# A new order of heavy and light steps, and a small product moved behind a larger one, in a two-layer hybrid decoder trunk

## The reference

```
swiglu(h, wg, wu, wd) = (silu(h @ wg) * (h @ wu)) @ wd
logits = t @ router ; top_v, top_i = top_k(logits, 2) ; top_w = softmax(top_v)
out = sum over experts e of combine[:, e] * swiglu(t, eg[e], eu[e], ed[e])
```

## Time and profile before

| | us |
|---|---|
| median of 3 runs | 1355.4 (1354.23 to 1355.93) |
| the profiled execution | 1358.07 |
| its span, first to last instruction | 1356.1 |
| TensorE busy in the span | 1307.8 |
| VectorE busy | 1139.9 |
| ScalarE busy | 945.6 |
| mean granted clock of TensorE | 0.987 of full |

### The profile page before, as it was taken

How to read it: one execution, slowest core, us unless ns; L and a number is a source line. 1 busy time by engine, 2 the same in 40 slices (tenths; PEclk the granted TensorE clock), 3 DMA queues, 4 the chain that set the end, 5 groups by cost and what they waited for, 6 DMA issues and landing times.

```text
span 1356.1 us, 17180 instructions
## 1 busy us (share of the span) xinstructions
PE 1307.8 (96%) x6502; PEld 1072.6 (79%) x6503; DVE 1139.9 (84%) x1045; ACT 945.6 (70%) x844; POOL 100.0 (7%) x67
## 2 busy tenths in 40 slices
PE   8999999999999999999999999999999999999984
PEld 5898888887898878788877887788887887878763
DVE  5767655556666899899998998999999899999997
ACT  4644444444744778688886887887888687888874
POOL 1140000000241100000000000000000000000030
PEclk9999999999999999999998999999999999999998
DMA  9434655552533899999999999999999999999993
GB/s 352 183 114 159 228 186 186 186 206 105 186 106 129 310 363 375 383 397 420 421 421 384 393 419 385 409 420 409 419 418 419 384 390 411 415 421 421 420 420 129
DMA packets 63028, 437.42 MB, mean 323 GB/s; under 512 B 7231, under 2 KB 7409, under 8 KB 11746
## 3 DMA queue, kind: packets, MB, share of 16 engines
q1 hardware_dynamic: 58896, 423.20, 78.2%
q0 software_dynamic: 3904, 13.06, 2.6%
q10 hardware_dynamic: 146, 0.07, 0.0%
HBM read 430.01 MB, written 6.29 MB: 322 GB/s over the span
## 4 chain that ended last, share of the span: by engine, by line
PE 72%; DVE 20%; ACT 3%; issue 3%; DMA 1%; DVEq 0%; ACTq 0%; SPq 0%
PE ps L2136 30%; PE ps L2160 15%; DVE w_lo L403 11%; PE ps L1824 4%; PE ps L2276 4%; PE ps L1839 4%; DVE spare_w L403 3%; PE ps L1927 3%; PE ps L2256 2%; ACT w_hi L398 2%; PE ps L1801 2%; DVE g_sb L1382 1%; DMA raw<-in_stream 1%; PE ps L2152 1%; PE ps L2196 1%
## 5 line engine op out<-in xcount | busy, mean ns | idle before, releaser
L403 DVE TENSOR_TENSOR w_lo<-raw,w_hi 128x2048 fp32r<-128x2048 f32 x313 | 715.2, 2298 | 108.6 <-ACT w_hi L398 107.8
L398 ACT ACTIVATE w_hi<-raw 128x2048 fp32r<-128x2048 f32 x315 | 599.2, 1912 | 150.2 <-PE ps L2160 58.3
L2136 PE MATMUL ps<-w_hi,xT_hi 128*128 128x512 f32 x564 | 224.4, 398 | 0.5 <-DVE xT_lo L1414 0.5
L2136 PE MATMUL ps<-w_lo,xT_hi 128*128 128x512 f32 x564 | 220.3, 391 | 0.0
L2136 PE MATMUL ps<-w_hi,xT_lo 128*128 128x512 f32 x564 | 219.9, 390 | 0.0
L403 DVE TENSOR_TENSOR spare_w<-raw,spare_w 128x2048 fp32r<-128x2048 f32 x85 | 193.9, 2281 | 14.8 <-ACT spare_w L398 14.6
L398 ACT ACTIVATE spare_w<-raw 128x2048 fp32r<-128x2048 f32 x85 | 162.6, 1913 | 27.1 <-PE ps L2160 22.4
L2136 PEld LDWEIGHTS ps<-w_hi,xT_hi 128*128 128x128 f32 x564 | 106.0, 188 | 22.7 <-DVE xT_lo L1414 0.7
L2136 PEld LDWEIGHTS ps<-w_lo,xT_hi 128*128 128x128 f32 x564 | 105.9, 188 | 22.5
L2136 PEld LDWEIGHTS ps<-w_hi,xT_lo 128*128 128x128 f32 x564 | 106.1, 188 | 20.8
L2160 PE MATMUL ps<-w_hi,aT_hi 128*128 128x512 f32 x288 | 115.5, 401 | 3.3 <-DVE w_lo L403 2.4
(11 more groups left out here) (355 smaller groups left out, 1932.2 us busy)
## 6 DMA issues: line engine op xcount, KB each, us to landing
raw<-in_stream SPq DMA_DIRECT2D x400, 1024.0 KB, 8.1
outs<-work POOLq DMA_DIRECT2D x5, 512.0 KB, 8.4
gain<-in_gains POOLq DMA_DIRECT2D x4, 512.0 KB, 5.2
h<-in_x SPq DMA_DIRECT2D x2, 512.0 KB, 6.5
raw<-in_stream SPq DMA_DIRECT2D x2, 512.0 KB, 6.1
tokens<-big POOLq DMA_DIRECT2D x2, 512.0 KB, 3.3
outs<-work POOLq DMA_DIRECT2D x4, 256.0 KB, 7.7
out<-work SPq DMA_DIRECT2D x4, 256.0 KB, 2.7
```

The source lines that it names most:

```text
L398: nc.scalar.activation(home(n, 0), raw[:, n % RAW, :], ACT.Copy).then_inc(hi_done, 1)
L403: nc.vector.tensor_tensor(home(n, 1), raw[:, n % RAW, :], home(n, 0).bitcast(F32), ALU.subtract).then_inc(lo_done, 1)
L2136: last = nc.tensor.matmul(ps[:, 4 + s, :], (xT_hi, xT_lo)[xp][:, k, x * P:(x + 1) * P], w((n + half), wp, kk * 512, (kk + 1) * 512), start ...
```

## The change

`TURNS` gets another order, from its 34th letter on (step 33). In the last steps, 49 to 55, the letters go from h l h l l l l to h l h h l l l; between steps 33 and 50 six light steps come one place earlier. By the rules above `END` of experts 3, 4 and 6 goes from 39, 51, 42 to 40, 52, 41, and `RETURN_AT` with it; `PLACE` of expert 4 goes from 35 to 36 and of expert 7 from 40 to 39; `BEGIN` of experts 4 and 7 from 40 and 44 to 41 and 43.

On TensorE, `gate_up_free` and `token_ids` move from between the two down products of the step to behind the second. On VectorE, the copy of the numbers moves from between the lo splits of units m+7 and m+8 to behind the latter. No instruction is added or removed.

```diff
-TURNS = "hhhhhlhhlhhlhhlhlhhlhhlhhlhhlhhlhhlhhlhhlhlhhlhlhhlhllll"
+TURNS = "hhhhhlhhlhhlhhlhlhhlhhlhhlhhlhhlhlhhlhhlhlhhlhlhlhlhhlll"
@@ VectorE, step(i)
                 lo_unit(dve, m + 7)
-                if i in IDS_AT:
-                    token_ids(IDS_AT[i])
                 if i == STEPS - 4:
                     last_slots()
                 if not ends:
                     lo_unit(dve, m + 8)
+                if i in IDS_AT:
+                    token_ids(IDS_AT[i])
@@ TensorE, expert_step(i)
                 if p < HEAVY:
                     down(fm, 1, B, 0, m + 4, 0, j == 0, False)
-                    if i in IDS_AT:
-                        gate_up_free(1, q, B + 2, i + 1)
-                        token_ids(IDS_AT[i])
                     down(fm, 1, B + 1, 1, m + 5, 0, False, final)
                 else:
                     light_down(B, 0, m + 4, j == 0, False)
-                    if i in IDS_AT:
-                        gate_up_free(1, q, B + 2, i + 1)
-                        token_ids(IDS_AT[i])
...
                     light_down(B + 1, 1, m + 5, False, final)
...
+                if i in IDS_AT:
+                    gate_up_free(1, q, B + 2, i + 1)
+                    token_ids(IDS_AT[i])
```

## The result

| | before | after |
|---|---|---|
| median of 4 runs, us | 1354.8 (1352.25 to 1355.93) | 1341.2 (1340.67 to 1343.19) |
| ratio | | 0.9905, 95% interval [0.9887, 0.9923] |
| profiled execution | 1358.07 | 1341.33 |
| its span | 1356.1 | 1339.4 |

The kernel is faster by 13.6 us between the medians, 12.9 by the ratio. The forecast was 1348.9, 6.5 less than the 1355.4 that it started from: the way was right, the size was less than half. A term of the sum was mis-sized, and it has to be found.

The account below looks back on a forecast made before the run. TensorE bounds until about 1130 through waits before L2297, the stream from 1188 on. Span 1356.1 - 16 + 8.0 + 1.5 = 1349.6 us, 6.5 less; off the median 1355.4 that gives 1348.9, range 1338 to 1359.

Parts of the forecast that it names:

- The moved product, gain 16 us: Token product behind the second down product: TensorE is offered 21.2 us, of which 16 reach the end (8 to 21).
- The cap read from the stream's lost rate: Time the weight stream lost against its undisturbed rate in the expert stage limits the gain to 18 to 21 us.
- the 2 us taken off: Deducted from the gain for short TensorE waits on weights, expected to appear as the slack goes.
- The clock as a term of its own: Slow TensorE clock in down products behind the waits before L2297: 8.0 of the 21.2 us offered.
- The copy on VectorE, 0: VectorE's copy behind the lo split of m+8: at most 1 us for seven copies, taken as 0.
- The new order of heavy and light, 0: Steps from 33 on: the stream already sets the pace and moves the same units, so taken as 0.
- The last heavy expert's return, +8.0: Return one step later: the last gather lands at 1337.4 and VectorE's first `combine` comes 8.0 us later (5.1 to 13.8).
- its clock, +1.5: TensorE stands during the late return, so its last products run at a lower clock: 1.5 us (0 to 3).
- The gathers come in time: Rival at the end: quick gathers, no clock loss, gain 18.5, cost 5.1, so 1342.0 us; chance 0.18.
- The stream did follow: Denies the rival that stalls go but VectorE becomes the bound: gain 6, cost 9.5, 1358.9 us; chance 0.11.
- the wait did not move: Denies the rival that the token product waits behind the second down product: gain about 5, 1359.9 us; chance 0.06.
- the return cost less than the waits gave: Denies the rival that the last return costs 16.8 us, more than the gain: 1358.2 us; chance 0.12.

Follow-up runs that it names:

- the pair alone: The kernel before with the token numbers' product and VectorE's copy moved, old order of steps kept: 1340.1 us (0.9888), again 1339.0 us (0.9883).
- the filled waits: The kernel before with nine small identity products issued ahead of TensorE's wait for bank 5, where a light step comes next: 1352.5 us, 0.9974.

## Why the prediction was right in its way and wrong in its size

*What bounds the kernel.* Right. TensorE was the bound until about 1130, the waits before L2297 were on its path, and the stream idled because of them.

*The moved product, gain 16 us.* Right: 15.2 and 15.9 measured for the pair alone. The cap read from the stream's lost rate, 17.8 to 20.9 (the upper end is 20.8 when redone), was a good way to size it. That the 2 us taken off led so near was in part luck: it stood for waits for split weights, which hardly grew, and 1.2 to 2.1 us came from the wait before L2305. The clock as a term of its own is shown by the filled waits, 3.5 us in the runs; that all of its 8.0 us were worth as much as the standing is not shown.

*The copy on VectorE, 0.* Right, as far as 0.9907 can tell.

*The new order of heavy and light, 0.* The late return in the old order costs as much (0.9914) as the new order does (0.9905, 0.9912), and the new order with another tail and the return at its old step (0.9897) can't be told from the old order (0.9888, 0.9883). So 0 stands, within the intervals. I missed one thing in it: with expert 4's next step heavy, one of the five waits goes by the order alone.

*The last heavy expert's return, +8.0, and its clock, +1.5.* This is the step that failed: the mechanism was right, the wait before `combine` came, of 7.25 us, but these two terms were sized at 9.5 us, and their price is 2 to 4 us in the runs. By the rows, against the pair moved alone, the first `combine` came only 2.1 us later:

- `y_copy` 14.1 us later, where I took 15.5;
- the last landing 5.75 us behind its issue (1306.84 to about 1312.6), where I took 7.5; the lower bound had been 5.2;
- what it is compared with had moved as well: beside the now unbroken stream the gathers took up to 16.3 us, where the kernel before had shown 14.1. I held the base fixed at the old trace's 14.1.

These three are 1.4, 1.8 and 2.2 us. Together with 0.6 us more slack of VectorE (1309.0 to 1310.56, before 0.9) they come to 6.0 us, which is, rounding apart, the 5.9 between 8.0 and 2.1. The same 2.1 us can be read from VectorE's side, and this explains what the prediction did not see: once the gathers come behind the stream they stop slowing it, its last unit was rounded 5.0 us earlier, VectorE was ready for `combine` at 1305.37 instead of 1310.56, 5.2 us earlier, and so 7.25 us of standing are worth 2.1.

The clock's 1.5 was 0. TensorE did stand 9.97 us and ran at half clock after it (a granted clock of 0.50 in 1317 to 1321):

```profile
1317.36 0.80 PE L2276 MATMUL ps<-w_hi,aT_hi 128*128 128x512 f32 x1 [9.97 <-DVE w_lo L403]
```

But from the first `combine` to the end of the span it is 26.8 us, 27.2 and 26.8 in the two profiles of the pair alone, and 26.7 before. With the pair alone the same products, behind a wait of 2.64 us, mostly ran at the lower clock too, and in the changed kernel VectorE works without a gap from its last two additions into what TensorE waits for.

*The rivals.* "The gathers come in time" (1342.0) was nearest, though the gathers did not come in time; their lateness was cheap, so its number is near by luck. The stream did follow, the wait did not move, and the return cost less than the waits gave. The rule for a 512 KB transfer in the Trainium skill, "DMA: Bandwidth & Descriptors", section "Anatomy of one DMA — SWDGE (gpsimd) path", about 3.2 us, gave an estimated cost of 5.6 instead of my 8.0. The quickest landing of 5.4 us, 0.94 of it the issue, leaves 4.5: nearer to the rule than to the rows of before that ran under load, but the rule's cost too is above the 2 to 4 measured.

## What to carry to other kernels

In a ring where TensorE, VectorE and the stream are all within 2% of their limit, most of a wait of one reaches the end (here 15 to 16 us of the 21.2 of standing and slow clock), and what the memory's rate falls short of its own undisturbed rate caps what it is worth (here 17.8). When a transfer moves from beside a saturated stream to behind it, price both: here it landed in about half the time, and the stream got back what the transfer took. A long wait that appears in the trace is no price by itself; compare the start of the instruction behind it with the same instruction in the kernel without the wait.

## What the runs showed of the hardware

How long GpSimd takes to issue the same indirect gather goes with what VectorE runs. The seven gathers of tokens (L571) in the kernel before, the changed kernel, and the one with the copy at the old place; duration min/median/max in ns:

```profile
L571 POOL DMA_INDIRECT small<-tokens,tok_i x7: 2743/2796/2852, 497.7 to 1133.9; - x7
```

```profile
L571 POOL DMA_INDIRECT small<-tokens,tok_i x7: 967/5605/5680, 498.9 to 1099.8; - x7
```

```profile
L571 POOL DMA_INDIRECT small<-tokens,tok_i x7: 2756/7799/7871, 499.0 to 1100.4; - x7
```

With VectorE standing it takes 0.94 us (the last two gathers of the changed kernel, at 1305.59 and 1306.84). Where a split already runs at its start, it ends 0.8 to 1.2 us behind the end of one to four splits of 2.3 us each: 2.8 us in the kernel before (issued at 548.35, the split ends at 550.27), 5.6 to 5.7 in the changed kernel in four of seven places and 7.8 in four of seven with the copy at its old place. A gather that starts 0.07 us ahead of a split (at 498.90 in the changed kernel) takes 0.97 beside it. The longest are 9.98 with filled waits and 10.03 with the last heavy step at 51.

The Trainium skill, "SBUF — State Buffer", section "SBUF: two separate sides", offers a cause: GpSimd writes the descriptors through a port pair that VectorE can hold for a whole instruction. The rows agree in that a gather waits for whole instructions. But of the form that the splits have, a tensor-tensor instruction with both inputs in SBUF, the same section says only that it contends with GpSimd's reads, and infers that it leaves the writing of descriptors free. Which it was here was not tried, so the cause stays open.

For the gathers of tokens it costs nothing: no instruction is listed as waiting for them (the one at 549.28 has its first transposes at 571.57, and the slowest landing was 13.7 us). At the end of the kernel it can, as with the filled waits, and need not: in the second run of the pair alone the last gather took 7.83 us to issue, and `combine` did not wait.

In the kernel before, TensorE stood 2.54, 2.58, 2.34, 2.35 and 2.58 us before L2297. After the first four the granted clock was 0.66, 0.50, 0.66 and 0.66 over 5 us, products at the lower of its two levels among them; after the fifth, at 1131, it was 1.00, though that stand was as long as any. Nine products of 0.24 us in the wait, which left stands of 0.3 to 0.6 us, kept it at 1.00 in all five places.
